# A two-block transformer on one core: loads of the mixing stage by first use, zeros written a stage earlier, and four units on VectorE's ring of banks

## The chip, the core and the metric

The kernel runs on one core of a Trainium2 chip. The metric is the device time of one execution in microseconds, lower is better. The profile is that of one execution on the same core.

## What is computed

Two layers of a first block (pooling in one, forgetting attention in the other, each with memory attention), and then a second block on the 1024 x 1024 rows `x`. The change lies in the second block. Cut to what matters there:

```python
h = _modulate(_rmsnorm(x, norm1_g[l]), shift1, scale1)
z = h @ w_in[l]
zu, zv, zr = jnp.split(z, [GMLP_WIDTH, 2 * GMLP_WIDTH], axis=-1)
y_a = _gmlp_mixer(zu, zv, gmlp_ln_w[l], gmlp_ln_b[l], gmlp_ws[l], gmlp_bs[l])
y_b = _rwkv7_mixer(zr, ...)
y = jnp.concatenate([y_a, y_b], axis=-1) @ w_out[l]
x = x + gate1[:, None, :] * y
h = _modulate(_rmsnorm(x, norm2_g[l]), shift2, scale2)
y = _hier_moe(h, router_group_w[l], ..., w_gate[l], w_up[l], w_down[l])
x = x + gate2[:, None, :] * y
```

`_rwkv7_mixer` is a scan over 1024 tokens with a 64 x 64 state for each of 8 heads. The kernel solves it in 16 chunks of 64 tokens: within a chunk a triangular system is inverted by levels, and between chunks the state goes through one product each. `_hier_moe` sends each token to 2 of 32 experts in blocks of 128 rows; 15 further blocks stand ready for experts with more than 128 rows, and the rows of those must read as zero where nobody writes them.

## The kernel before

The program is a sequence of stages with a barrier between them (`E.run`). Three matter here.

**The RWKV stage** (`stage_rwkv_pairs`) goes over four pairs of heads, c = 0 to 3. A list `script`, written once and walked by every engine, sets the order: for each pair `turn` (transposes), `A` (five chunkwise products), `AV`, five levels of the inversion, and `tail`. Between the levels of pair c stand the steps that prepare pair c + 1 (`front`): three projections, `small`, and after the fifth level `sums`, whose part on VectorE is a chain of 11 operations. So on VectorE `sums` of pair c + 1 stands ahead of `tail` of pair c. In `tail` TensorE makes GH (the solved rows, four banks), MT (two banks, L1640), N (two banks, L1648 and L1649), Q (two banks, L1657) and Yi (two banks, L1664 and L1665).

Apart from that the stage computes the gMLP columns `zu, zv` in 32 *units* of 128 rows by 256 columns (L1575), each 8 matmuls of 128 x 256. The table `fill` puts them at places of the script, one of them at ("GH", c), behind the four GH banks and ahead of MT, and one at ("N", c), behind N. ScalarE copies each unit out of PSUM to `uv_rows` (L1885), SyncE stores it (L1706).

PSUM's eight banks are two rings of four (`class Ring`): `ringA`, mostly emptied by ScalarE, and `ringD`, emptied by VectorE. Banks are handed out in turn; a `take` waits until the take four before it has been freed, and `free` counts in order:

```python
before = self.n - len(self.banks)
return self.banks[self.at[key] % len(self.banks)], (before if before > 0 else None)
```

GH, Yi and all units use `ringA`; MT, N and Q use `ringD`. GH takes all four banks of `ringA`, so the unit behind it waits for ScalarE's first GH copy (L1908); MT waits for the last.

**The mixing stage** (`stage_mix`) works on blocks of 128 tokens, t = 0 to 7, in a software pipeline of NT + 5 rounds: in round t the two state products of block t (`chain`, L2146, reading `s_mt`), then `mix` and `rwkv_rows` of block t - 1, `turn` of t - 2, `out` of t - 3 (the product with `w_out`, L2188 to L2190), norm and router behind. Six streams (`s_uv`, `s_mt`, `s_n`, `s_qt`, `s_yi`, `s_v`) and the rows `x` are loaded for each block, two buffers each. All DMAs are issued by SyncE in program order: first `ws` and the parameters, then blocks 0 and 1, then `w_o` (4 MB), then the zeros for the 15 further expert blocks (L2277, 7680 KB to `y_slots`), then the streams of block 2. VectorE and TensorE wait once, at the start, for the sum of all parameters. GpSimd splits `w_o` into a high and a low part by eight casts (L2301) and eight subtractions (L2303); `out(0)` waits for all.

**The expert stage** follows and reads the weights.

Of the kernel before, what the change touches and what calls it, by code (L numbers as in the profile page):

```python
# [15 lines left out]
P = 128  # L16
D = 1024
# [1287 lines left out]
UVW = 256  # L1305

# [97 lines left out]
def stage_rwkv_pairs(nc, E, A):  # L1404
# [14 lines left out]
    with ExitStack() as st:  # L1419
# [57 lines left out]
        assert sum(fill.values()) == len(units)  # L1477
# [19 lines left out]

        chunks = [(t, slice(q * C, (q + 1) * C)) for t in range(NT) for q in range(2)]
        of = lambda t: slice(t * C, (t + 1) * C)

        with nc.Block() as block:

            @block.tensor
            def _(pe):
# [61 lines left out]
                turns = iter(units)  # L1566

                def fill_(*at_):
                    for _ in range(fill.get(at_, 0)):
                        q, t = next(turns)  # L1570
                        if t == 0:
                            pe.wait_ge(uv_landed, 16 * (q + 1))
                        bank = take(ringA, ("uv", q, t))
                        for d in range(ND):
                            last = nc.tensor.matmul(bank[:, 0:UVW], E.hT[:, d, t * P:(t + 1) * P], w_uv[:, d, :],  # L1575
                                                    start=(d == 0), stop=(d == ND - 1))
                        last.then_inc(ringA.full, 1)
# [97 lines left out]
            def _(sp):  # L1675
# [16 lines left out]
                turns = iter(units)  # L1692

# [5 lines left out]
                def fill_(*at_):  # L1699
                    for _ in range(fill.get(at_, 0)):  # L1700
                        q, t = next(turns)
# [3 lines left out]
                        sp.wait_ge(ringA.free, ringA.nth(("uv", q, t)))  # L1705
# [28 lines left out]
                steps = {"proj": proj, "turn": turn, "A": a_part, "tail": tail, "fill": fill_}  # L1734
# [3 lines left out]
                sp.wait_ge(S_["stored"], 64 * NPAIR)  # L1738
                for i in range(2):
# [4 lines left out]
            def _(pool):  # L1744
# [23 lines left out]

                done(nc.gpsimd.memset(blocksum[:], 1.0))
# [37 lines left out]
            def _(act):  # L1807
# [68 lines left out]
                turns = iter(units)  # L1876

                def fill_(*at_):
                    for _ in range(fill.get(at_, 0)):
                        q, t = next(turns)  # L1880
# [23 lines left out]
                def tail(c):  # L1904
# [4 lines left out]
                    fill_("GH", c)  # L1909
# [12 lines left out]
            def _(dve):  # L1922
# [145 lines left out]
def stage_mix(nc, E, A, rows_in, rows_out, normed_out, y_slots):  # L2068
# [5 lines left out]
    ZW = 256  # L2074
    H = GW // HD
    NR = N_GROUPS + EXPERTS
    with ExitStack() as st:
# [29 lines left out]
        zeros, zeros_set, zeroed = sb("zeros", [P, ZW]), E.sem("zeros_set"), E.sem("slots_zeroed")  # L2107
        w_landed = {x: E.sem("mix_" + x) for x in ("o", "ws", "row")}
# [17 lines left out]
        with nc.Block() as block:  # L2126

            @block.tensor
            def _(pe):
# [63 lines left out]
                def router(t):  # L2193
                    pe.wait_ge(ringA.free, ringA.nth(("t", t, 1)))
                    bank = take(ringD, ("r", t))
# [4 lines left out]
                pe.wait_ge(sems["tril"], 1)  # L2200
                for h in range(2):
                    bank = take(ringA, ("ws", h))
                    for k in range(4):
                        last = nc.tensor.transpose(bank[:, k * P:(k + 1) * P], ws[:, 4 * h + k, :], E.ident[:])
                    last.then_inc(ringA.full, 1)
                pe.wait_ge(small, 16 * 6)
                for t in range(NT + 5):
                    if t < NT:
                        chain(2 * t)
                        chain(2 * t + 1)  # L2210
                    if 1 <= t <= NT:
                        mix(t - 1)
                        rwkv_rows(t - 1)
# [12 lines left out]
            def _(sp):  # L2226
                sp.dma_start(ws[:], A["gmlp_ws_2"][0].rearrange("h t s -> t h s")).then_inc(w_landed["ws"], 16)
                sp.dma_start(bs[:], A["gmlp_bs_cols"]).then_inc(small, 16)
                sp.dma_start(g2[:], A["rwkv_g2_2"][0]).then_inc(small, 16)
                sp.dma_start(rw[:, :, 0:N_GROUPS], A["router_group_w_2"][0].rearrange("(c p) n -> p c n", p=P)).then_inc(small, 16)  # L2230
# [957 lines left out]
```

## Time and profile before

| what | value |
|---|---|
| median of 3 runs | 3264.18 us (3259.43 to 3264.87) |
| the profiled execution | 3260.56 us, span of the profile 3258.8 us |
| TensorE busy | 2914.8 us, 89% of the span |
| VectorE busy | 1735.0 us, 53% |
| ScalarE busy | 1083.0 us, 33% |
| GpSimd busy | 410.1 us, 13% |
| mean granted TensorE clock | 0.936 |
| RWKV stage, mixing stage, expert stage | first DMA at 1666, 2249 and 2516 us |

Times in the views are microseconds from the span's start. PE is TensorE's matmuls, PEld its weight loads, DVE VectorE, ACT ScalarE, POOL GpSimd, SPq the DMA issues of SyncE. The granted clock is a share of 2.4 GHz: 1.00 is that level, 0.50 is 1.2 GHz. A bracket behind a row of the timeline says how long the engine idled before it and for whom.

### The profile page before, as it was taken

How to read it: one execution, taken by the hardware profiler on the slowest of the kernel's cores; microseconds unless marked ns; L12 is line 12 of the kernel's file. 1: busy time of each engine (PE TensorE's matmuls, PEld its weight loads, DVE VectorE, ACT ScalarE, POOL GpSimd, SP SyncE). 2: the span in 40 equal slices, each digit the busy share in tenths (PEclk: the TensorE clock that was granted, in tenths of full speed). 3: DMA queues.
4: the chain of work that ended last, by engine and by line, in shares of the span. 5: the costliest groups of instructions: out<-in, count | busy, mean ns of one | idle time of the engine just before them, and what ended most of it. 6: DMA issues, size and time to landing. Idle time of an engine off the chain costs nothing. (4 is left out here: it accounts for less than half of the span.)

```text
span 3258.8 us, 45746 instructions
## 1 busy us (share of the span) xinstructions
PE 2914.8 (89%) x18548; PEld 2082.4 (64%) x18548; DVE 1735.0 (53%) x2733; ACT 1083.0 (33%) x1690; POOL 410.1 (13%) x334
## 2 busy tenths in 40 slices
PE   7999899898699999998989999996598599999991
PEld 5877544544477777764436677686477477777770
DVE  2223323464356666662325435262665799999984
ACT  2111100122245555451222212132233365666652
POOL 1322000000222222210021010110300000000001
PEclk9999999899799999999989999998688799999995
DMA  4111031652222112113111021014533699999985
GB/s 152 49 42 42 2 140 45 188 182 65 65 59 59 52 53 59 53 33 129 52 55 37 23 68 60 10 56 155 199 120 117 235 398 399 397 399 397 398 310 223
DMA packets 290277, 454.32 MB, mean 139 GB/s; under 512 B 15616, under 2 KB 157440, under 8 KB 290096
## 3 DMA queue, kind: packets, MB, share of 16 engines
q1 hardware_dynamic: 283040, 426.05, 37.3%
q0 software_dynamic: 7056, 25.69, 2.0%
q8 instruction: 133, 2.18, 0.3%
q14 instruction: 48, 0.39, 0.0%
HBM read 389.77 MB, written 61.93 MB: 139 GB/s over the span
## 5 line engine op out<-in xcount | busy, mean ns | idle before, releaser
L677 PE MATMUL psum<-wo,yT 128*128 128x512 f32 x768 | 337.7, 601 | 15.7 <-DMA wo<-in_w_out 15.7
L677 PEld LDWEIGHTS psum<-wo,yT 128*128 128x128 f32 x768 | 147.3, 193 | 196.7 <-issue 180.1
L910 PE MATMUL psum<-x_hi,w_hi 128*128 128x512 f32 x512 | 212.0, 414 | 29.3 <-POOL w_lo L1011 28.6
L1100 DVE TENSOR_TENSOR fox_pT_lo<-psum,fox_pT_hi 128x512 fp32r<-128x512 f32 (+2 forms) x192 | 107.2, 558 | 183.4 <-ACT fox_pT_hi L1039 174.2
L912 PE MATMUL psum<-x_hi,w_lo 128*128 128x512 f32 x512 | 202.0, 394 | 0.0
L911 PE MATMUL psum<-x_lo,w_hi 128*128 128x512 f32 x512 | 201.0, 393 | 0.0
L2797 ACT CAST hi_d<-land_d 128x2048 fp32r<-128x2048 f32 x66 | 122.7, 1908 | 140.1 <-PE psum L2669 140.1
L1526 PE MATMUL psum<-hT,wr 128*128 128x512 f32 x384 | 167.1, 594 | 0.0
L1009 POOL CAST w_hi<-w_land 128x1024 fp32r<-128x1024 f32 x48 | 49.8, 1037 | 909.7 <-DMA w_land<-in_w_in 509.9
L2942 DVE TENSOR_TENSOR lo_d<-land_d,hi_d 128x2048 fp32r<-128x2048 f32 x66 | 148.3, 2289 | 21.5 <-ACT hi_d L2797 21.5
L162 PE MATMUL psum<-x_hi,w_hi 128*128 128x512 f32 x384 | 151.9, 396 | 8.7 <-POOL w_lo L153 8.7
L163 PE MATMUL psum<-x_lo,w_hi 128*128 128x512 f32 x384 | 151.2, 394 | 0.0
L739 DVE SCALAR_TENSOR_TENSOR x_tile<-x_tile,psum 128x512 f32<-128x512 f32 x32 | 22.0, 688 | 242.2 <-PE psum L677 241.7
L2942 DVE TENSOR_TENSOR lo_g<-land_g,hi_g 128x2048 fp32r<-128x2048 f32 x66 | 150.9, 2288 | 0.0
L164 PE MATMUL psum<-x_hi,w_lo 128*128 128x512 f32 x384 | 150.7, 392 | 0.0
L1050 ACT ACTIVATE fox_p<-fox_p,fox_bias 128x256 f32<-128x256 f32 (+7 forms) x128 | 99.6, 778 | 119.9 <-DVE fox_bias L1086 116.3
L1575 PE MATMUL psum<-w_uv,hT 128*128 128x256 f32 x512 | 124.8, 400 | 10.1 <-ACT GH L1908 9.8
L1526 PEld LDWEIGHTS psum<-hT,wr 128*128 128x128 f32 x384 | 72.8, 191 | 87.9 <-issue 87.4
L910 PEld LDWEIGHTS psum<-x_hi,w_hi 128*128 128x128 f32 x512 | 97.1, 190 | 47.9 <-POOL w_lo L1011 30.1
L2797 ACT CAST hi_g<-land_g 128x2048 fp32r<-128x2048 f32 x66 | 125.2, 1898 | 0.8 <-DMA land_g<-in_moe_w_gate 0.8
L2667 PE MATMUL psum<-hi_d,e_h_hi 128*128 128x512 f32 x264 | 117.2, 444 | 6.7 <-DVE e_h_lo L2959 6.7
L1083 DVE CUSTOM_DVE_ANT_0 fox_p<-psum,ncum 128x256 f32<-128x256 f32 (+7 forms) x128 | 97.0, 758 | 48.8 <-PE psum L929 40.2
(482 smaller groups left out, 6435.5 us busy)
## 6 DMA issues: line engine op xcount, KB each, us to landing
land_g<-in_moe_w_gate SPq DMA_DIRECT2D x66, 1024.0 KB, 7.6
land_u<-in_moe_w_up SPq DMA_DIRECT2D x66, 1024.0 KB, 7.5
land_d<-in_moe_w_down SPq DMA_DIRECT2D x66, 1024.0 KB, 9.1
ada<-in_ada_w SPq DMA_DIRECT2D x24, 1024.0 KB, 5.2
y_slots<-yb SPq DMA_DIRECT2D x33, 512.0 KB, 10.0
w<-in_w_in SPq DMA_DIRECT2D x24, 512.0 KB
wo<-in_w_out SPq DMA_DIRECT2D x12, 1024.0 KB
w_land<-in_w_in SPq DMA_DIRECT2D x24, 512.0 KB, 3.8
```

Source lines behind the costliest of these rows:

```text
L162: self.nc.tensor.matmul(bank[:], hi[:, d, :], E.x_hi[:, d, cols], start=(d == 0), stop=False)
L163: self.nc.tensor.matmul(bank[:], hi[:, d, :], E.x_lo[:, d, cols], start=False, stop=False)
L164: last = self.nc.tensor.matmul(bank[:], lo[:, d, :], E.x_hi[:, d, cols], start=False, stop=(d == ND - 1))
L677: last = nc.tensor.matmul(banks[hf][:], E.yT[:, c, t * P:(t + 1) * P], wo[:, c, hf * HALF:(hf + 1) * HALF], start=(c == 0), stop=(c == NY ...
L910: nc.tensor.matmul(bank[:], hi[:, d, :], E.x_hi[:, d, cols], start=(d == 0), stop=False)
L911: nc.tensor.matmul(bank[:], hi[:, d, :], E.x_lo[:, d, cols], start=False, stop=False)
L912: last = nc.tensor.matmul(bank[:], lo[:, d, :], E.x_hi[:, d, cols], start=False, stop=(d == ND - 1))
L1526: last = nc.tensor.matmul(bank[:], w[m % NW][:, d, :], E.hT[:, d, hf * HALF:(hf + 1) * HALF], start=(d == 0), stop=(d == ND - 1))
L1575: last = nc.tensor.matmul(bank[:, 0:UVW], E.hT[:, d, t * P:(t + 1) * P], w_uv[:, d, :], start=(d == 0), stop=(d == ND - 1))
L2667: nc.tensor.matmul(bank, hi_t, hi_w, start=start, stop=False)
L2797: nc.scalar.copy(w_hi[x][:], land[x][:]).then_inc(hi_set[x], 1)
L2942: V.tensor_tensor(w_lo[x][:], land[x][:], w_hi[x][:].bitcast(F32), ALU.subtract).then_inc(lo_set[x], 1)
```

## The change

1. *Mixing stage, loads.* SyncE issues them in another order: streams `n`, `mt`, `uv` of block 0, `ws`, the gMLP norm's rows, and so on; `w_o` behind the streams of block 1, then the gate, the two `x` blocks and the router's parameters. The waits for parameters are split by semaphore and stand in front of the first use. TensorE's transposes of `ws` and ScalarE's copies of them stand behind the first round's own work.
2. *Zeros.* The memset and the write of the zeros move to the RWKV stage. The write is cut into four parts of 1920 KB; SyncE issues one at the fifth level of each pair.
3. *Unit at ("GH", c).* It takes a bank of `ringD` instead of `ringA`, and VectorE copies it out at the head of its `tail` instead of ScalarE. There are four such units.

The table `units_at` only writes down which units stand at which place; the assignment is the same as before.

```diff
...
+        units_at = {at_: [next(turns) for _ in range(fill.get(at_, 0))] for at_ in places}
...
                 def fill_(*at_):
-                    for _ in range(fill.get(at_, 0)):
-                        q, t = next(turns)
+                    ring = ringD if at_[0] == "GH" else ringA
+                    for q, t in units_at[at_]:
                         if t == 0:
                             pe.wait_ge(uv_landed, 16 * (q + 1))
-                        bank = take(ringA, ("uv", q, t))
+                        bank = take(ring, ("uv", q, t))
...
+                def level(c, m):
+                    if m == LEVELS:
+                        if c == 0:
+                            sp.wait_ge(zeros_set, 1)
+                        part = further[:, c * ZEROS:(c + 1) * ZEROS, :]
+                        sp.dma_start(part, zeros[:].rearrange("p (o n) -> p o n", o=1).broadcast_to([P, ZEROS, ZW])).then_inc(zeroed, 16)
...
@@ scalar, tail @@
                             nc.scalar.copy(GH[:, j, 4 * th:4 * th + 4, :], bank.rearrange("p (t n) -> p t n", t=4)).then_inc(ringA.free, 1)
-                    fill_("GH", c)
                     fill_("N", c)
@@ vector, tail @@
+                    for q, t in units_at["GH", c]:
+                        n = q * NT + t
+                        dve.wait_ge(ringD.full, ringD.nth(("uv", q, t)))
+                        if n >= 2:
+                            dve.wait_ge(uv_stored[n % 2], 16 * (n // 2))
+                        V.tensor_copy(uv_rows[n % 2][:], ringD.bank(("uv", q, t))[:, 0:UVW]).then_inc(ringD.free, 1)
                     for q in range(2):
                         dve.wait_ge(ringD.full, ringD.nth(("MT", c, q)))
@@ stage_mix, tensor @@
-                pe.wait_ge(small, 16 * 6)
                 for t in range(NT + 5):
                     if t < NT:
                         chain(2 * t)
                         chain(2 * t + 1)
+                    if t == 0:
+                        turn_ws()
                     if 1 <= t <= NT:
+                        if t == 1:
+                            pe.wait_ge(ringA.free, ringA.nth(("ws", 1)))
                         mix(t - 1)
+                        if t == 1:
+                            pe.wait_ge(small, 32)
                         rwkv_rows(t - 1)
@@ stage_mix, sync @@
-                sp.wait_ge(zeros_set, 1)
-                further = y_slots[EXPERTS * P:SLOTS, :].rearrange("(p b) d -> p (b d)", p=P).rearrange("p (k n) -> p k n", n=ZW)
-                sp.dma_start(further, zeros[:].rearrange("p (o n) -> p o n", o=1).broadcast_to([P, OVER * D // ZW, ZW])).then_inc(zeroed, 16)
...
+                for x in ("n", "mt", "uv"):
+                    load(x, 0)
+                sp.dma_start(ws[:], A["gmlp_ws_2"][0].rearrange("h t s -> t h s")).then_inc(w_landed["ws"], 16)
+                rows(ln_w, "gmlp_ln_w_2", "ln")
+                rows(ln_b, "gmlp_ln_b_2", "ln")
+                load("qt", 0)
...
@@ stage_mix, vector @@
-                dve.wait_ge(w_landed["row"], 16 * 5)
-                dve.wait_ge(small, 16 * 6)
                 V.memset(T[0][:], 0.0).then_inc(sems["T"], 1)
```

How the order changes on the engines. VectorE at the end of a pair of heads (here the first), where `at<-at,lw` is the last operation of the next pair's front, `L<-psum,ident` the two MT banks, `COPY L` the two N banks and `L<-psum,r` the two Q banks. Before:

```order
L1987 TENSOR_TENSOR r<-r,cl 128x1024
L1989 SCALAR_TENSOR_TENSOR at<-at,lw 128x1024
L2035 TENSOR_TENSOR L<-psum,ident 128x8x64 x2
L2039 COPY L<-psum 128x8x64 x2
L2042 TENSOR_TENSOR L<-psum,r 128x8x64 x2
```

And with the change:

```order
L1998 TENSOR_TENSOR r<-r,cl 128x1024
L2000 SCALAR_TENSOR_TENSOR at<-at,lw 128x1024
L2049 COPY uv_rows<-psum 128x256
L2052 TENSOR_TENSOR L<-psum,ident 128x8x64 x2
L2056 COPY L<-psum 128x8x64 x2
L2059 TENSOR_TENSOR L<-psum,r 128x8x64 x2
```

The copy of the unit stands behind the front and ahead of the MT banks.

SyncE in the RWKV stage with the change, from the last weight load of the first pair's levels to that pair's stores:

```order
L1698 DMA wr<-in_w_in 128x8x128 x3
L1745 DMA y_slots<-zeros 128x15x256
L1712 DMA uv_rows_dram<-uv_rows 128x256
L1703 DMA w_uv<-in_w_in 128x8x256
L1712 DMA uv_rows_dram<-uv_rows 128x256
L1733 DMA mt<-L 128x1024
```

The row with the zeros is new; the others stood in this order before.

SyncE in the mixing stage, around `w_o`. Before:

```order
L2256 DMA s_qt<-qt 128x4x128
L2253 DMA s_yi<-yi_rows 128x512
L2253 DMA s_v<-v_rows 128x512
L2262 DMA x_1<-x_rows 128x1024
L2274 DMA w_o<-in_w_out 128x8x1024
L2277 DMA y_slots<-zeros 7680x1x256
L2253 DMA s_uv<-uv_rows_dram 128x1024
L2256 DMA s_mt<-mt 128x4x128
```

And with the change:

```order
L2266 DMA s_v<-v_rows 128x512
L2302 DMA w_o<-in_w_out 128x8x1024
L2303 DMA gate<-gate_rows_dram 128x1024
L2275 DMA x_0<-x_rows 128x1024
L2275 DMA x_1<-x_rows 128x1024
L2306 DMA rw<-in_router_group_w 128x8x4
L2307 DMA rw<-in_router_expert_w 128x8x32
L2308 DMA rb<-in_router_group_b 128x4
L2309 DMA rb<-in_router_expert_b 128x32
L2266 DMA s_uv<-uv_rows_dram 128x1024
L2269 DMA s_mt<-mt 128x4x128
```

The last two rows of each are the streams of block 2. What stands between `w_o` and them is the zeros before, and the gate, the two `x` blocks and the router's parameters now.

## Rows read from the trace of the kernel before

**Rows 1.** Busy time by stretch; after the engines: PEclk, DMA share, GB/s.
```profile
1734.00:2249.00 515.00, 493.11 (x7962) 378.71 (x7960) 233.97 (x251) 121.83 (x210) 58.95 (x40) 0.99 0.14 44
2249.00:2265.00 16.00, 1.97 (x8) 1.57 (x8) 0.27 (x1) 2.45 (x3) 1.42 (x2) 0.50 0.85 219
2265.00:2285.00 20.00, 11.47 (x98) 9.19 (x98) 12.34 (x26) 7.25 (x10) 0.00 (x0) 0.50 1.07 384
2285.00:2311.00 26.00, 0.13 (x2) 0.13 (x4) 8.50 (x8) 1.29 (x3) 23.07 (x14) 0.50 1.06 367
```
**Rows 2.** Timeline of TensorE, start of the mixing stage: start us, us, what.
```profile
2310.87 1.12 PE L2146 MATMUL psum<-T,s_mt 64*64 64x64 f32 x16 [26.52 <-DMA s_mt<-mt]
...
2341.83 0.78 PE L2188 MATMUL psum<-w_o_hi,y2T_hi 128*128 128x512 f32 x1
```
**Rows 3.** Timeline of SyncE's DMA issues, start of the mixing stage.
```profile
2249.38 0.38 SPq L2227 DMA_DIRECT2D ws<-in_gmlp_ws  x1
...
2270.96 0.68 SPq L2274 DMA_DIRECT2D w_o<-in_w_out  x1
...
2273.37 29.43 SPq L2253 DMA_DIRECT2D s_uv<-uv_rows_dram  x1
```
**Rows 4.** DMA issues by line: count, KB each, median us to landing.
```profile
y_slots<-zeros SPq DMA_DIRECT2D x1, 7680.0 KB, 36.7
...
ws<-in_gmlp_ws SPq DMA_DIRECT2D x1, 512.0 KB, 4.3
```
**Rows 5.** TensorE's waits, 1734 to 2249 us: us in total, times, longest.
```profile
PE psum L1575 <- ACT GH L1908: 9.8, 3, 3.3
```
**Rows 6.** Timeline of TensorE, tail of pair 0.
```profile
1863.03 5.41 PE L1575 MATMUL psum<-w_uv,hT 128*128 128x256 f32 x16 [3.27 <-ACT GH L1908]
...
1869.88 0.28 PE L1648 MATMUL psum<-GH,tok_b 64*64 64x64 f32 x2
...
1873.75 3.72 PE L1575 MATMUL psum<-w_uv,hT 128*128 128x256 f32 x16
1877.40 1.73 PE L1657 MATMUL psum<-rbT,GH 64*64 64x64 f32 x58
```
**Rows 7.** Timeline of VectorE, tail of pair 0.
```profile
1876.52 1.28 DVE L2035 TENSOR_TENSOR L<-psum,ident 128x512 f32<-128x512 f32 x2
```
**Rows 8.** Timeline of VectorE: an operation on 128x256 that reads PSUM.
```profile
2312.13 0.42 DVE L2369 TENSOR_TENSOR T<-psum,s_n 128x256 f32<-128x256 f32 x1 [18.28 <-PE psum L2146]
```
**Rows 9.** Timelines of VectorE and TensorE, tails of pairs 1 and 2.
```profile
2000.61 6.77 PE L1575 MATMUL psum<-w_uv,hT 128*128 128x256 f32 x16 [3.27 <-ACT GH L1908]
...
2014.10 1.28 DVE L2035 TENSOR_TENSOR L<-psum,ident 128x512 f32<-128x512 f32 x2
...
2016.28 1.73 PE L1657 MATMUL psum<-rbT,GH 64*64 64x64 f32 x58
...
2140.32 5.20 PE L1575 MATMUL psum<-w_uv,hT 128*128 128x256 f32 x16 [3.27 <-ACT GH L1908]
...
2153.82 1.28 DVE L2035 TENSOR_TENSOR L<-psum,ident 128x512 f32<-128x512 f32 x2
...
2154.55 1.74 PE L1657 MATMUL psum<-rbT,GH 64*64 64x64 f32 x58
```
**Rows 10.** Timeline of GpSimd: first and last of 16 operations that split `w_o`.
```profile
2287.37 1.04 POOL L2301 CAST w_o_hi<-w_o 128x1024 fp32r<-128x1024 f32 x1 [32.53 <-DMA w_o<-in_w_out]
...
2313.41 2.41 POOL L2303 TENSOR_TENSOR w_o_lo<-w_o,w_o_hi 128x1024 fp32r<-128x1024 f32 x1
```
**Rows 11.** Timeline of VectorE beside GpSimd's split, block 0.
```profile
2287.43 1.51 DVE L2413 TENSOR_TENSOR y<-y,gn_w 128x512 f32<-128x512 f32 x1
2288.98 2.71 DVE L2414 TENSOR_TENSOR s_v<-s_v,gn_b 128x512 f32<-128x512 f32 x1
2291.73 1.41 DVE L2415 TENSOR_TENSOR y<-y,s_v 128x512 f32<-128x512 f32 x1
```
**Rows 12.** Timeline of VectorE with GpSimd quiet, block 2.
```profile
2344.28 0.69 DVE L2414 TENSOR_TENSOR s_v<-s_v,gn_b 128x512 f32<-128x512 f32 x1
```

More of the change, by code:

```diff
@@ L1305 @@
 UVW = 256
+ZW = 256
 class Modulation:
@@ L1699, in fill_ @@
                 def fill_(*at_):
-                    for _ in range(fill.get(at_, 0)):
-                        q, t = next(turns)
+                    ring = ringD if at_[0] == "GH" else ringA
+                    for q, t in units_at[at_]:
                         if t == NT - 1 and q + 1 < 2 * GW // UVW:
@@ L1874, in turn @@
                     nc.scalar.copy(E.bonus[:, :, 2 * c:2 * c + 2], bank[:, 0:2 * NT].rearrange("p (t j) -> p t j", t=NT)).then_inc(ringA.free, 1)
-                turns = iter(units)
                 def fill_(*at_):
-                    for _ in range(fill.get(at_, 0)):
-                        q, t = next(turns)
+                    for q, t in units_at[at_]:
                         n = q * NT + t
@@ L2106, in stage_mix @@
         small = E.sem("mix_small")
-        zeros, zeros_set, zeroed = sb("zeros", [P, ZW]), E.sem("zeros_set"), E.sem("slots_zeroed")
-        w_landed = {x: E.sem("mix_" + x) for x in ("o", "ws", "row")}
+        w_landed = {x: E.sem("mix_" + x) for x in ("o", "ws", "ln", "gn", "gate", "router")}
         x_landed = [E.sem(f"x2_landed{i}") for i in range(NX)]
@@ L2198, in router, with turn_ws @@
                     last.then_inc(ringD.full, 1)
[L2200 to L2205, printed above, removed]
-                pe.wait_ge(small, 16 * 6)
+                def turn_ws():
+                    pe.wait_ge(sems["tril"], 1)
+                    for h in range(2):
+                        bank = take(ringA, ("ws", h))
+                        for k in range(4):
+                            last = nc.tensor.transpose(bank[:, k * P:(k + 1) * P], ws[:, 4 * h + k, :], E.ident[:])
+                        last.then_inc(ringA.full, 1)
                 for t in range(NT + 5):
@@ L2273, in _ @@
+                for x in ("qt", "yi", "v"):
+                    load(x, 1)
+                sp.dma_start(w_o[:], A["w_out_2"][0].rearrange("(c p) n -> p c n", p=P)).then_inc(w_landed["o"], 16)
+                sp.dma_start(gate[:], E.gates[:, 0:D]).then_inc(w_landed["gate"], 16)
+                for t in range(NX):
                     load_x(t)
-                sp.dma_start(w_o[:], A["w_out_2"][0].rearrange("(c p) n -> p c n", p=P)).then_inc(w_landed["o"], 16)
-                sp.wait_ge(zeros_set, 1)
@@ L2293, in _ @@
             def _(pool):
-                nc.gpsimd.memset(zeros[:], 0.0).then_inc(zeros_set, 1)
                 pool.wait_ge(w_landed["ws"], 16)
@@ L2309, in got @@
                     return ringA.bank(key)
-                for h in range(2):
-                    nc.scalar.copy(wsT[:, 4 * h:4 * h + 4, :], got(("ws", h)).rearrange("p (h n) -> p h n", h=4)).then_inc(ringA.free, 1)
                 for t in range(NT + 5):
@@ L2323, in _ @@
                         nc.scalar.activation(gdev[:], mv_[:, 1:2], ACT.Sqrt, bias=E.eps_ln[:]).then_inc(sems["dev"], 1)
+                    if t == 0:
+                        for h in range(2):
+                            nc.scalar.copy(wsT[:, 4 * h:4 * h + 4, :], got(("ws", h)).rearrange("p (h n) -> p h n", h=4)).then_inc(ringA.free, 1)
                     if 1 <= t <= NT:
```

69 lines of the change are left out of this document (44 added, 25 removed).

## The prediction

> **What bounds the kernel now.** I read the busy time by stretch first. From 1734 to 2249 us, the stage that solves the RWKV chunks, TensorE works 493 of 515 us at almost full clock, while the DMA engines are used to 0.14 [rows 1]: time that TensorE loses there is lost to the kernel. I then read TensorE's timeline where the mixing stage begins. It computes 128 tokens (a block) at a time. The third block's state product starts at 2310.87 us after 26.52 us of idling for `s_mt`, and the first product with `w_out` at 2341.83 us [rows 2]. SyncE's timeline says why: its first DMA of the stage goes out at 2249.38 us, `w_o` at 2270.96, the zeros behind it, and the third block's `s_uv` then sits 29.43 us in the issue [rows 3]. The zeros are 7680 KB and land 36.7 us after their issue [rows 4]. So this gap is the DMA queue's, and behind it everything up to the first `w_out` product is late.
>
> The third view is TensorE and VectorE beside each other at the end of a pair of heads. In three of the four pairs TensorE idles for ScalarE's GH copies before the unit behind the solved rows, 9.8 us in all [rows 5]. Pair 0: the unit starts at 1863.03 after 3.27 us of idling, the two N banks follow from 1869.88, the next unit at 1873.75 and Q at 1877.40 [rows 6]. VectorE at that time is in the next pair's front, which stands ahead of this tail in its program, and takes up the first MT bank only at 1876.52 [rows 7].
>
> **The change part by part.**
>
> *Unit behind the solved rows on ringD.* The unit no longer waits for ScalarE's GH copies, so it moves up by 3.3 us per pair. But `ringD` has four banks, and the takes are now unit, MT, MT, N, N: the second N bank is the fourth take after the unit and gets the unit's bank. It is free only once VectorE has copied it, and VectorE comes to that copy after the front, where it used to come to MT. Queued behind the waiting N matmuls on TensorE are the next unit, Q and Yi. The copy of 128x256 out of PSUM costs about 0.42 us by the nearest row [rows 8]. Pair 0: the copy ends at 1876.52 + 0.42 = 1876.94, N's second bank starts at about 1877.05 with 0.1 for the signal, one N bank takes (1873.75 - 1869.88) / 2 = 1.9 us, the unit 3.65 us, and Q starts at 1882.6 instead of 1877.40: 5.2 us late. What ScalarE gives back is swallowed by the same wait. Pairs 1 and 2 by the same sum from 2014.10 and 2153.82: Q at 2020.2 instead of 2016.28, and 2159.9 instead of 2154.55, so 3.9 and 5.3 us [rows 9]. Pair 3 has no next front and its unit did not idle: 0. Sum 14.4 us.
>
> To this comes the clock. After an idle stretch of 3.27 us the same unit took 5.41, 6.77 and 5.20 us instead of 3.72 [rows 6, 9], 6.2 us over the three pairs. The new idle stretch is longer, 9 to 10 us: without its own idling the unit starts at 1859.8, and with 3.65 us for it, 1.4 for MT (1863.03 + 5.41 to 1869.88) and 1.9 N's first bank ends at 1866.8 at the earliest, the second starts at 1877. No row shows an idle stretch of this length in this stage, so I bound it: 0 if the clock holds, and N's 1.9 plus the unit's 3.7 at half clock, 5.6 a pair or 16.8, if it is low all through. I take the 6.2 of the nearest rows. Term: **+20.6 us**, between 14.4 and 31.
>
> *Zeros in the RWKV stage.* Four writes of 1920 KB, 5.4 us each at the 367 GB/s of the stretch in which the old one ran [rows 1]. They go out at each pair's fifth level, into queues used to 0.14; the next transfers that anyone waits for are the tail's stores, over 10 us later. Cost 0; without that cover it would be up to 5.4 us a pair. The memset moves ahead of the masks on GpSimd: 0.3 us at most, and not on TensorE's path.
>
> *Mixing stage, loads.* In bytes: ahead of and with `w_o` stand two blocks of streams (3584 KB), `ws` 512, four parameter rows 1024, `g2` 192 and `w_o` 4096, together 9.63 MB, at the 384 GB/s of the stretch 2265 to 2285 [rows 1] 25.1 us. The first transfer landed 4.3 us after its issue [rows 4], of which 1.4 us are its bytes, so 2.9 us of latency come on top: `w_o` lands 28 us after the stage's first DMA. Gate, two x rows and the router's weights (1.7 MB, 4.5 us), the third block's `s_uv` and `s_mt` (2.0 us), and 4 us for the router's small pieces follow (an estimate: the first 16 us moved 219 GB/s [rows 1], 6.9 us less than at 384, of which 2.9 are the latency). The third block then starts at about 39 us instead of 2310.87 - 2249.38 = 61.5: **22.5 us** earlier, with 3 us either way. The first blocks gain too (VectorE waited for all the parameter rows before), but blocks 0 and 1 are then done near 30 us and stand before the same gate, so that gain is not counted again.
>
> *What the earlier `w_o` brings with it.* GpSimd splits `w_o` for 28.5 us, from 2287.37 to 2315.8 [rows 10]. Before, TensorE and VectorE mostly idled meanwhile. Now the split runs from 28 to 57 us or more, and the third block works from 39 us beside it. VectorE's operations with both inputs in SBUF suffer there: three in a row took 1.51, 2.71 and 1.41 us [rows 11], and the middle one takes 0.69 us with GpSimd quiet [rows 12]: 1.2 us more each on average. A block has 12 such operations; some 9 fall before the split's end: 10.8 us, less 1 us that the old third block already lost. I take 10, between 4 and 16. The Trainium skill (SBUF — State Buffer, "Who interferes with whom") says that such an instruction and one of GpSimd that reads SBUF exclude each other for a whole instruction; taken at its worst, a wait of a whole GpSimd instruction each time, it gives the rival "locked" below.
>
> After the first `w_out` product the order of work is the same and a block costs what it did. Term: 22.5 - 10 = **-12.5 us**, between -5 and -21.
>
> **Sum:** 20.6 - 12.5 = +8.1 us. The profiled execution took 3260.56 us around a span of 3258.8 and would take 3268.7; the median of the runs, 3264.18, lies 3.6 us higher. I forecast the median: 3272 us, slower by 0.25%. From no change a measurement of this kernel can tell about 0.2%, 6.5 us.
>
> **The rivals.**
> *Undisturbed split.* VectorE's waits for GpSimd fall where it would have waited for TensorE or ScalarE anyway, and the third block loses next to nothing. It decides from about 0.2 us a conflicting operation. Then 20.6 - 22.5 = -1.9: 3262 us, and with a clock that holds -8: 3256. For it: the conflict is seen on three operations only. Against: VectorE is the engine that is waited for in a block.
> *The unit's move works as drawn.* Were the second N bank not held (VectorE reaching the copy in time), the 9.8 us of idling go and nothing comes: -9.8 - 12.5 = -22: 3242 us. Against it stand 1876.52, 2014.10 and 2153.82 [rows 7, 9], each some 10 us later than N's second bank could start (1866.8 in pair 0).
> *Cold TensorE.* The longer idle keeps the clock at half for N and the unit: +31 - 12.5 = 18.5: 3283 us. For it: the three old units differ by 1.6 us in what they lost.
> *Locked.* Each of the 9 operations waits out a mean GpSimd instruction, 28.5 / 16 = 1.8 us: 16 instead of 10 us, 3278 us.
>
> **How the numbers follow.** Forecast 0.45, undisturbed split 0.24, works as drawn 0.09, cold 0.11, locked 0.11. The predicted time is that of the forecast. The range, 3257 to 3284, holds the forecast's bounds, "cold" and "locked" and most of "undisturbed", and leaves out "works as drawn" and the tails. Slower by over 0.2%: three quarters of the forecast's case, cold and locked, 0.56. Within: the rest of the forecast's and three quarters of "undisturbed", 0.29. Faster: 0.15.
>
> **What would show it.** In the profile after: the unit behind the solved rows follows the solve without idling; the second half of N waits for the VectorE copy of `uv_rows`, some 9 us in each of pairs 0 to 2, and none in pair 3; ScalarE's idle before N does not matter. No zeros in the mixing stage, the third block's product some 39 us after the stage's first DMA, the first `w_out` product some 79 us after it (92.5 before). VectorE's operations in the third block stretched up to 2.7 us. I am wrong if N shows no wait, or if the RWKV stage is not longer by 14 us or more, or if the mixing stage up to the first `w_out` product shrinks by less than 5 or more than 21 us.

## The result, and the profile after

The changed kernel takes 3275.22 us (median of 7 runs, 3270.87 to 3276.2) and the kernel before, on the same chip, 3264.08 us (7 runs, 3259.43 to 3267.55): ratio 1.0033, 95% interval 1.0022 to 1.0045. It is slower, by 11 us where 8 were forecast. The profiled execution took 3275.86 us around a span of 3274.1. Of the kernel before, one execution in the third group of experiments took 4819.97 us at a granted clock of 0.587; it is left out everywhere.

From the first DMA of one stage to the first of the next, the two traces differ like this:

| stretch | before | after | difference | forecast |
|---|---|---|---|---|
| up to the RWKV stage | 1666.3 | 1663.8 | -2.5 | 0 |
| RWKV stage | 583.1 | 608.9 | +25.8 | +20.6 |
| mixing stage, up to the first `w_out` product | 92.45 | 80.1 | -12.4 | -12.5 |
| from that product to the first expert DMA | 173.9 | 178.2 | +4.3 | 0 |
| expert stage and the rest | 743.1 | 743.2 | +0.1 | 0 |

TensorE's waits in the RWKV stage of the changed kernel (us in total, times, longest):

```profile
PE psum L1656 <- DVE uv_rows L2049: 26.5, 3, 8.9
...
PE psum L1648 <- ACT GH L1920: 3.0, 3, 1.1
```

The 9.8 us of waiting for GH [rows 5] are down to 3.0, and 26.5 us of waiting for VectorE's copy of the unit stand in their place, three times, as forecast. TensorE and VectorE in the tail of pair 0 (start, length, operation, in brackets the idle time before it and its releaser):

```profile
1856.29 3.72 PE L1583 MATMUL psum<-w_uv,hT 128*128 128x256 f32 x16
...
1873.58 0.49 PE L1656 MATMUL psum<-GH,tok_b 64*64 64x64 f32 x4 [8.85 <-DVE uv_rows L2049]
...
1877.24 5.56 PE L1583 MATMUL psum<-w_uv,hT 128*128 128x256 f32 x16
1882.73 1.73 PE L1665 MATMUL psum<-rbT,GH 64*64 64x64 f32 x58
```
```profile
1871.97 1.23 DVE L2000 SCALAR_TENSOR_TENSOR at<-at,lw 128x1024 f32<-128x1024 f32 x1
1873.11 0.42 DVE L2049 COPY uv_rows<-psum 128x256 f32<-128x256 f32 x1
1873.44 1.28 DVE L2052 TENSOR_TENSOR L<-psum,ident 128x512 f32<-128x512 f32 x2
1874.64 0.68 DVE L2056 COPY L<-psum 128x512 f32<-128x512 f32 x1
```

Compare [rows 6, 7]. The unit ends at 1860.0, and its bank is copied at 1873.11, when the last operation of the next pair's front (L2000) is through. The copy takes the 0.42 us that were assumed. The second bank of N then takes 3.66 us (1873.58 to 1877.24) where a bank took 1.9 before, and the next unit 5.56 instead of 3.72. The granted clock over these two and after them (busy time of TensorE, its weight loads, VectorE, ScalarE, GpSimd, then PEclk, DMA share, GB/s); it is at the lower level, 0.50 or 1.2 GHz, over all of N's bank, at 0.66 on average over the unit, and back at 2.4 GHz by 1884:

```profile
1873.50:1876.90 3.40, 3.32 (x62) 3.32 (x63) 1.82 (x4) 0.00 (x0) 0.00 (x0) 0.50 0.13 43
1877.30:1882.70 5.40, 5.40 (x17) 4.22 (x16) 0.69 (x1) 0.00 (x0) 0.00 (x0) 0.66 0.00 0
1884.00:1889.00 5.00, 5.00 (x149) 5.00 (x146) 1.31 (x2) 0.58 (x1) 0.00 (x0) 1.00 0.78 236
```

In the mixing stage the third block's state product and the first product with `w_out` come 41.6 and 80.1 us behind the stage's first DMA at 2272.67 (61.5 and 92.45 before, [rows 2]):

```profile
2314.28 1.12 PE L2161 MATMUL psum<-T,s_mt 64*64 64x64 f32 x16 [16.51 <-DMA s_mt<-mt]
...
2352.76 0.78 PE L2203 MATMUL psum<-w_o_hi,y2T_hi 128*128 128x512 f32 x1
```

SyncE no longer sits behind the zeros [rows 3], but on the router's weights, and the third block's `s_uv` goes out 35.6 us into the stage:

```profile
2293.71 10.16 SPq L2307 DMA_DIRECT2D rw<-in_router_expert_w  x1
2303.92 3.87 SPq L2308 DMA_DIRECT2D rb<-in_router_group_b  x1
...
2308.31 0.43 SPq L2266 DMA_DIRECT2D s_uv<-uv_rows_dram  x1
```

GpSimd's split runs from 31.5 to 60.5 us of the stage, and VectorE's operations of the third block beside it are stretched, as in [rows 11]:

```profile
2304.20 1.04 POOL L2330 CAST w_o_hi<-w_o 128x1024 fp32r<-128x1024 f32 x1 [21.26 <-DMA w_o<-in_w_out]
...
2330.85 2.34 POOL L2332 TENSOR_TENSOR w_o_lo<-w_o,w_o_hi 128x1024 fp32r<-128x1024 f32 x1
```
```profile
2319.52 2.23 DVE L2412 TENSOR_SCALAR vn<-vg,g_mv,g_rstd 128x512 f32<-128x512 f32 x1
2321.79 1.40 DVE L2415 TENSOR_TENSOR vn<-vn,gln_w 128x512 f32<-128x512 f32 x1
2323.23 2.72 DVE L2416 TENSOR_TENSOR vn<-vn,gln_b 128x512 f32<-128x512 f32 x1
...
2331.30 1.92 DVE L2437 TENSOR_SCALAR gn_s<-gn_s 128x8 f32<-128x8 f32 x1
```

The four parts of the zeros land 9.1 us (median) after their issue; none of TensorE's longest waits in the RWKV stage is for them.

### The profile page after: what moved, and what is told of

Read it like the earlier page. It is cut to its first block and busy times, and to the rows that moved or that the text cites. A ratio compares the mean times of both kernels' runs of the same rounds, so it can differ in the third digit from the quotient of the medians.

```text
span 3274.1 us, 45754 instructions
## 1 busy us (share of the span) xinstructions
PE 2922.9 (89%) x18548; PEld 2086.6 (64%) x18548; DVE 1741.4 (53%) x2737; ACT 1081.9 (33%) x1686; POOL 411.5 (13%) x334
```

## The experiments

The theory (A): the unit's place on `ringD` costs the RWKV stage all it lost, since its copy stands behind VectorE's front; the zeros bring nearly all that the mixing stage gained. Eleven kernels were run, in three groups (e1 to e4, e5 to e8, e9 to e11), each group on another chip and with its own runs of the kernel before, whose medians were 3262.91, 3262.61 and 3260.15 us. Across groups the ratios are to be compared, and the medians only roughly. A letter names a rival within its own experiment: rival D of e2 and rival D of e6 are different ones.

| run | median us | ratio to before, 95% | RWKV stage | third block | first `w_out` product |
|---|---|---|---|---|---|
| before | | | 583.1 | 61.5 | 92.4 |
| after | 3275.22 | 1.0033 (1.0022 to 1.0045) | 608.9 | 41.6 | 80.1 |
| e1 order and zeros | 3251.44 | 0.9964 (0.9951 to 0.9977) | 585.7 | 41.3 | 79.9 |
| e2 unit alone | 3290.33 | 1.0081 (1.0063 to 1.0099) | 608.0 | 61.1 | 92.0 |
| e3 zeros alone | 3252.99 | 0.9972 (0.9960 to 0.9983) | 588.6 | 40.4 | 84.2 |
| e4 order alone | 3264.84 | 1.0004 (0.9993 to 1.0016) | 584.0 | 63.2 | 93.7 |
| e5 router late | 3245.67 | 0.9953 (0.9940 to 0.9966) | 582.7 | 38.3 | 78.9 |
| e6 unit's copy in front | 3258.03 | 0.9985 (0.9976 to 0.9994) | 589.0 | 41.6 | 79.8 |
| e7 three copies in front | 3237.27 | 0.9924 (0.9911 to 0.9937) | 576.1 | 42.3 | 79.9 |
| e8 no subtractions | 3241.80 | 0.9939 (0.9926 to 0.9952) | 582.2 | 41.2 | 71.7 |
| e9 casts on ScalarE | 3242.21 | 0.9949 (0.9933 to 0.9964) | 581.7 | 40.7 | 75.1 |
| e10 unit on ringA, copies in front | 3246.97 | 0.9959 (0.9944 to 0.9974) | 578.9 | 41.5 | 80.0 |
| e11 all | 3234.46 | 0.9929 (0.9911 to 0.9946) | 570.8 | 38.5 | 76.1 |

The last three columns are from one profiled execution each: the length of the stage, and the start behind the mixing stage's first DMA.

**e1.** The changed kernel, its third part undone.
```diff
-                    ring = ringD if at_[0] == "GH" else ringA
+                    ring = ringA
@@ scalar, tail @@
+                    fill_("GH", c)
                     fill_("N", c)
@@ vector, tail @@
-                    for q, t in units_at["GH", c]:
...
-                        V.tensor_copy(uv_rows[n % 2][:], ringD.bank(("uv", q, t))[:, 0:UVW]).then_inc(ringD.free, 1)
```


> The changed kernel with one of its three parts undone: the unit behind the solved rows goes back to ScalarE's ring and ScalarE's copy, in all four pairs. Load order, split waits and zeros stay as changed. Theory A (the 26.5 us that TensorE waits for VectorE's copy of that unit, with the slower clock behind each wait, is what the RWKV stage lost): from the stage's first DMA to the mixing stage's it takes 583 us again (608.9 in the changed kernel, 583.1 before), the three waits of 8.85 us on VectorE's uv_rows copy are gone, w_out's first product stays about 80 us behind the mixing stage's first DMA, and the kernel takes 3275.2 - 25.8 = 3249 us, 0.995 of the kernel before (3245 to 3254). Rival B (the zeros' four DMAs inside the RWKV stage cost part of the 25.8 us): the stage keeps 588 to 600 us and the total stays at 3254 to 3266. Rival C (the mixing stage's gain is given back once the stage runs into the experts without the slack upstream): total over 3258.

**e2.** The kernel before with that part alone (one line of several; SyncE's, ScalarE's and VectorE's go with it).
```diff
-                        bank = take(ringA, ("uv", q, t))
+                        bank = take(ring, ("uv", q, t))
```


> The kernel before with only the unit behind the solved rows moved to VectorE's ring and VectorE's copy; loads, waits and zeros as before. Theory A: the RWKV stage takes 609 us (583.1 before), three waits of about 9 us on VectorE's copy, the mixing stage as before (first product of w_out 92 us behind the stage's first DMA), total 3264.1 + 25.8 = 3290 us (3286 to 3293), ratio 1.008. Rival D (the unit on VectorE's ring does what it is drawn to do, and the loss came with the zeros or the new waits): 3252 to 3264 us, ratio 0.997 to 1.000.

TensorE's waits in the RWKV stage, e1 and then e2:
```profile
PE psum L1583 <- ACT GH L1920: 9.8, 3, 3.3
```
```profile
PE psum L1653 <- DVE uv_rows L2037: 26.6, 3, 8.9
```
Both came out by theory A within 3 us: e1 is 11.5 us faster than before, e2 27.4 us slower. The unit on `ringD` costs the RWKV stage 23.2 us with the rest of the change (608.9 against 585.7) and 24.9 us without it (608.0 against 583.1), and rivals B, C and D of these two fall. The two other parts are a gain of 0.36%, which the third more than eats.

**e3, e4.** The zeros alone, and the order of the loads with the split waits alone. In e4 the zeros are issued here:
```diff
                 sp.dma_start(rb[:, N_GROUPS:NR], A["router_expert_b_2"].broadcast_to([P, EXPERTS])).then_inc(w_landed["router"], 16)
+                sp.wait_ge(zeros_set, 1)
...
+                sp.dma_start(further, zeros[:].rearrange("p (o n) -> p o n", o=1).broadcast_to([P, OVER * D // ZW, ZW])).then_inc(zeroed, 16)
```


> The kernel before with only the zeros moved: written in four parts by the RWKV stage, gone from the mixing stage; the mixing stage's loads keep their old order and its waits are the old joint ones. Theory A (the 7680 KB of zeros in front of the second block's streams were what held the mixing stage): the third block's first product is 40 to 44 us behind the stage's first DMA (61.5 before, 41.6 in the changed kernel), w_out's first product at 80 to 86 us (92.5 before, 80.1 changed), total 3264.1 minus 6 to 12 = 3252 to 3258 us. Rival E (the order of the loads and the split waits bring at least half of the mixing stage's gain): the first product of w_out at 86 us or later, total 3259 or more.

> The kernel before with only the mixing stage's loads in order of first use and the waits split; the zeros stay in the mixing stage, as the last load ahead of the second block's streams, and the unit on ScalarE's ring. Theory A (order and split waits move work only inside the time that the zeros take anyway): the third block's first product at 58 to 64 us behind the stage's first DMA, w_out's first product at 88 to 95 us, total 3261 to 3266 us. Rival E (they bring at least half of the gain): w_out's first product at 86 us or less, total under 3259.

The third block's product and the first `w_out` product in e3 (its stage begins at 2256.27) and e4 (2253.24):
```profile
2296.64 1.12 PE L2156 MATMUL psum<-T,s_mt 64*64 64x64 f32 x16 [6.02 <-DMA s_mt<-mt]
...
2340.45 0.78 PE L2198 MATMUL psum<-w_o_hi,y2T_hi 128*128 128x512 f32 x1
```
```profile
2316.46 1.12 PE L2145 MATMUL psum<-T,s_mt 64*64 64x64 f32 x16 [38.74 <-DMA s_mt<-mt]
...
2346.94 0.78 PE L2187 MATMUL psum<-w_o_hi,y2T_hi 128*128 128x512 f32 x1
```
Both came out by theory A, and rival E falls. The zeros alone bring 9.9 us. The order alone brings nothing that can be told: e4 has its first blocks done earlier and then idles 38.74 us where the kernel before idled 26.52. On top of the moved zeros the order gets the first `w_out` product from 84.2 to 79.9 us, but e1 and e3 differ in the median by 1.6 us only, less than can be told apart.

**e5.** e1, and the router's four loads behind the third and fourth block's streams.
```diff
-                sp.dma_start(rw[:, :, N_GROUPS:NR], A["router_expert_w_2"][0].rearrange("(c p) n -> p c n", p=P)).then_inc(w_landed["router"], 16)
...
+                    if t == 2:
...
+                        sp.dma_start(rw[:, :, N_GROUPS:NR], A["router_expert_w_2"][0].rearrange("(c p) n -> p c n", p=P)).then_inc(w_landed["router"], 16)
```


> The run with order and zeros as changed and the unit back on ScalarE's ring, and in it the router's four loads issued two blocks later, behind the third and fourth block's streams. In the changed kernel SyncE issues the router's expert weights for 10.16 us and its group bias for 3.87 us, and the third block's uv_rows only behind them, 35.6 us after the stage's first DMA. Theory A (the router's small pieces hold SyncE and so the third block's streams): the third block's first product moves from 41.3 us to about 36 us behind the stage's first DMA, w_out's first product from 79.9 us to 75 to 78 us, total 3246 to 3250 us against 3251.4 of that run. Rival F (the streams then only meet GpSimd's split and the queue elsewhere): w_out's first product stays at 79 to 81 us, total within 2 us of 3251.4.

```profile
2269.38 1.28 SPq L2261 DMA_DIRECT2D s_uv<-uv_rows_dram  x1
2270.71 1.39 SPq L2264 DMA_DIRECT2D s_mt<-mt  x1
...
2273.17 9.66 SPq L2264 DMA_DIRECT2D s_qt<-qt  x1
```
SyncE, from the stage's start at 2248.78, now issues `s_uv` at 20.6 us and sits 9.66 us on another stream, `s_qt` of the same block. So a hold of this length does not need the small pieces of the router; what decides where SyncE is held no run shows. Nor is the hold what the third block waits for in the main: its `s_mt` goes out 21.9 us into the stage and not 35.9 as in e1, 14.0 us earlier, but the product that waits for it starts only 3.0 us earlier (38.3 against 41.3). The first `w_out` product comes 1.0 us earlier (78.9), between the two theories, and the median, 3245.67, lies just below theory A's range. It is 5.8 us below e1, but each is compared with its own runs of before, and the two ratios' intervals overlap: unclear.

**e6.** The changed kernel; in pairs 0 to 2 the unit's copy stands in the middle of the next pair's front.
```diff
@@ vector, sums @@
                     link(dve, V.reciprocal(tmp[:], tmp[:]))
+                    if c > 0:
+                        unit_out(c - 1)
@@ vector, tail @@
-                    for q, t in units_at["GH", c]:
...
+                    if c == NPAIR - 1:
+                        unit_out(c)
```


> The changed kernel with one thing moved: in pairs 0 to 2 VectorE copies the unit behind the solved rows in the middle of the next pair's front, right behind the reciprocal, and not behind the whole front. Same instructions, same rings. Theory A (N's second bank waits only because the copy that frees it stands at the end of VectorE's front): the three waits of 8.85 us before N go, N runs at the fast clock in 1.9 us; Q now waits 3 to 5 us for VectorE's MT copy, as the unit did for GH in the kernel before. The RWKV stage takes 580 to 586 us (608.9 changed, 583.1 before), total 3248 to 3254 us, like the run with the unit on ScalarE's ring. Rival D (the ring of four banks itself is too short with one unit more in it): the stage stays over 595 us and the total over 3262 us.

**e7.** e6, and the MT and N copies too.
```diff
                     link(dve, V.tensor_tensor(K[:], K[:], rate[:], ALU.mult))
+                    if c > 0:
+                        mt_out(c - 1)
...
                     link(dve, V.tensor_tensor(K[:], K[:], e2[:], ALU.mult))
+                    if c > 0:
+                        n_out(c - 1)
```


> The run before, and VectorE's MT and N copies of pairs 0 to 2 stand in the next pair's front too (MT behind k's scaling by the rate, N behind k's product with e). Theory A (behind the solved rows the bound is VectorE's order, since Q waits for the MT copy behind the front): Q starts some 5 us earlier in each of three pairs, the front ends 3 us later, the RWKV stage takes 568 to 578 us, total 3236 to 3248 us. Rival G (the next pair's front is what bounds each pair's end, and lengthening it by 3 us costs what Q gains): the stage takes 580 to 590 us, total 3248 to 3258 us.

**e10.** e7, with the unit back on `ringA` and ScalarE's copy; MT and N stay in the front.
```diff
-                    ring = ringD if at_[0] == "GH" else ringA
+                    ring = ringA
@@ vector, sums @@
-                    if c > 0:
-                        unit_out(c - 1)
```


> The run with VectorE's unit, MT and N copies in the next pair's front (3237.3 us), and in it the unit behind the solved rows goes back to ScalarE's ring and ScalarE's copy; the MT and N copies stay in the front. Theory A (the ring change is worth its 9.8 us of TensorE waiting for GH copies, as the change has it, as soon as VectorE's copies no longer stand behind the front): the three waits of 3.3 us on ScalarE's GH copy come back, the RWKV stage takes 583 to 588 us against 576.1, total 3244 to 3250 us. Rival I (the gain came from the moved MT and N copies alone, and the ring does nothing, because what TensorE waits less there it waits more at the next front): the stage takes 574 to 579 us, total 3234 to 3241 us.

The longest of TensorE's waits for another engine in the RWKV stage, in e6, e7 and e10:
```profile
PE psum L1665 <- DVE L L2059: 12.2, 3, 4.1
```
```profile
PE psum L1648 <- ACT GH L1920: 3.2, 3, 1.1
```
```profile
PE psum L1583 <- ACT GH L1920: 9.5, 3, 3.3
```
Q's first 58 products in pair 0 of e6:
```profile
1875.81 2.99 PE L1665 MATMUL psum<-rbT,GH 64*64 64x64 f32 x58 [4.05 <-DVE L L2059]
```
VectorE in pair 0 of e7, front and copies interleaved:
```profile
1859.84 6.55 DVE L2012 RECIPROCAL tmp<-tmp 128x1024 f32<-128x1024 f32 x1
1866.42 0.42 DVE L1985 COPY uv_rows<-psum 128x256 f32<-128x256 f32 x1
...
1871.44 1.29 DVE L1994 TENSOR_TENSOR L<-psum,ident 128x512 f32<-128x512 f32 x2
...
1875.22 1.29 DVE L2001 COPY L<-psum 128x512 f32<-128x512 f32 x2
```
In e6 the wait before N is gone with nothing changed but the copy's place, so e6's rival D falls: the ring is long enough, the order of VectorE was the fault. But the stage, 589.0 us, is 3 us longer than expected and the median, 3258.03 (0.9985), 4 us above the range. Q waits 4.05 us for the MT copy, which also stands behind the front. That wait was expected; not expected was that it costs clock as well: Q's first 58 products take 2.99, 3.00 and 3.00 us in the three pairs instead of 1.73, 3.8 us in all. In e7 no wait for another engine over 1.1 us is left there, rival G falls, and the kernel is at 0.9924 of the one before, 25 us faster; the changed one was at 1.0033.

e10 puts a price on the unit's ring: with the MT and N copies in the front the unit on `ringA` brings 9.5 us of waiting for GH back, and the kernel stands at 0.9959 (0.9944 to 0.9974) against e7's 0.9924 (0.9911 to 0.9937), 9.7 us in the medians. The total is theory A's; the stage is not: 578.9 us where theory A had 583 to 588 and rival I 574 to 579. The 576.1 of e7 that both were reckoned from was a long one: e11 has the same RWKV code and took 570.8, 8.1 us less than e10 (last section). So by the total, and by e11's stage, rival I falls, and the third part of the change is a gain of its own once VectorE's order fits it. The moved MT and N copies by themselves, e10 against e1, show no clear gain: 0.9959 against 0.9964, with intervals that overlap.

**e8.** e1; GpSimd writes zeros where it subtracted.
```diff
-                    nc.gpsimd.tensor_tensor(w_o_lo[:, d, :], w_o[:, d, :], w_o_hi[:, d, :].bitcast(F32), ALU.subtract).then_inc(wo_split, 1)
+                    nc.gpsimd.memset(w_o_lo[:, d, :].bitcast(F32), 0.0).then_inc(wo_split, 1)
```


> The run with order and zeros as changed and the unit on ScalarE's ring, and in it GpSimd sets w_out's low part to zero where it subtracted before, so the low part of w_out is left out of the product. Theory A (GpSimd's eight subtractions of 2.34 us stretch VectorE's operations of the third block: 2.72 us against 0.69 us): the split ends 8 to 12 us earlier, VectorE's stretched operations of that block go back to 0.42 to 0.69 us apart from those beside the casts, w_out's first product moves from 79.9 us to 70 to 76 us behind the stage's first DMA, total 3242 to 3248 us. Rival F (the block is bound by its streams' landing and the chain of TensorE and VectorE, the stretch only fills waits): w_out's first product stays at 78 to 80 us, total 3249 to 3252 us.

**e9.** e1; the casts on ScalarE.
```diff
@@ gpsimd @@
-                    nc.gpsimd.tensor_copy(w_o_hi[:, d, :], w_o[:, d, :]).then_inc(wo_hi_set, 1)
@@ scalar @@
+                    if t == 2:
+                        act.wait_ge(w_landed["o"], 16)
+                        for d in range(ND):
+                            nc.scalar.copy(w_o_hi[:, d, :], w_o[:, d, :]).then_inc(wo_hi_set, 1)
```


> The run with order and zeros as changed and the unit on ScalarE's ring (3251.4 us), and in it ScalarE makes the eight casts of w_out, in the idle time before the third block's gelu, and GpSimd only the eight subtractions. Theory A (what is left of the split beside the third block costs the block its stretch; the run without subtractions had w_out's first product at 71.7 us against 79.9): the split ends 51 to 54 us behind the stage's first DMA (some 60 there), VectorE's operations behind that are back at 0.4 to 0.7 us, w_out's first product at 74 to 77 us, total 3245 to 3249 us. Rival H (ScalarE's casts hold back its gelu of the third block, or stretch as VectorE's operations do): w_out's first product at 79 us or later, total 3250 or more.

VectorE's operations of the third block in e8 beside GpSimd (the casts run until 2291.5), and ScalarE and GpSimd in e9:
```profile
2290.61 1.40 DVE L2410 TENSOR_TENSOR vn<-vn,gln_w 128x512 f32<-128x512 f32 x1
2292.05 0.69 DVE L2411 TENSOR_TENSOR vn<-vn,gln_b 128x512 f32<-128x512 f32 x1
...
2294.28 0.69 DVE L2421 TENSOR_TENSOR y<-y,gu 128x512 f32<-128x512 f32 x1
```
```profile
2274.01 7.67 ACT L2338 CAST w_o_hi<-w_o 128x1024 fp32r<-128x1024 f32 x8 [4.08 <-DMA w_o<-in_w_out]
```
```profile
2275.20 19.32 POOL L2326 TENSOR_TENSOR w_o_lo<-w_o,w_o_hi 128x1024 fp32r<-128x1024 f32 x8 [21.88 <-ACT w_o_hi L2338]
```
With the third block starting at the same time (41.2 and 41.3 us), the first `w_out` product comes 8.2 us earlier in e8: that is the contention on the third block, less what the casts left of it in e8. e8 leaves the low part of `w_out` out of the product and is no kernel to keep. In e9 the split ends at 51.3 us and 4.7 of the 8.2 us are gained; the median, 3242.21, is 3 us under theory A's range. By the place of the first `w_out` product and by the totals rival F of e8 and rival H fall; whether e9 is faster than e1 is not shown, since the two ratios' intervals overlap.

**e11.** e7, e5 and e9 together.

> All that gained, together: the changed kernel with VectorE's unit, MT and N copies in the next pair's front, the router's loads two blocks later, and w_out's casts on ScalarE. If the gains lie in different stages and add up: RWKV stage 574 to 578 us, w_out's first product 73 to 77 us behind the stage's first DMA, total 3237.3 minus 1 to 4 (router) minus 2 to 6 (casts) = 3228 to 3235 us. If later router loads and ScalarE's casts get in each other's way (the third block's uv_rows lands about when the casts run): w_out's first product at 78 us or later, total 3236 or more.

The first `w_out` product came out (76.1 us), the RWKV stage was 3 us under its range (570.8, see below), and the median, 3234.46, lies within its range and is the lowest of all. But against its own runs of before it stands at 0.9929, e7 at 0.9924: what router and casts add to e7 can't be told from nothing here. In its one trace the later router loads bring nothing on top of the casts: the third block starts at 38.5 us as in e5, but the first `w_out` product comes at 76.1 and not at e9's 75.1. The best version is e7 or e11, 25 to 26 us faster than before.

## Why the prediction was right, point by point

- *N waits for VectorE's copy in pairs 0 to 2, "some 9 us" each, none in pair 3.* Right: 8.85 us three times. e1 and e2 show that it is this part of the change that costs, e6 that the place of the copy does it.
- *14.4 us for the later Q.* Right. From the end of the solved rows' product to Q it took 17.6, 18.9 and 17.5 us before and 26.4, 26.7 and 25.7 after, 24.8 us more in all. Take from that what the clock took after the change (next point), 10.6 us, and 14.2 are left; the 6.2 us of slow clock in the units of before were part of Q's old place in the forecast's sum too. The other 1.0 us of the stage's 25.8 lies elsewhere.
- *6.2 us for the clock, from the units behind 3.27 us of idling.* This is the mis-sized term of the sum. N's second bank took 3.66 instead of 1.9 us three times, and the units 5.56, 5.85 and 5.11 instead of 3.72: 5.3 + 5.4 = 10.6 us. e2 repeats it behind its own three waits: the bank 3.7 us each time, the units 5.62, 5.68 and 5.06. The bounds (0 and 16.8) held it. The nearest rows were of a unit that itself began behind a wait; here N's second bank stands between the wait and the unit and is slowed as well, 5.3 us that those rows don't have. Why the unit behind it was still slow for a part no run shows.
- *Zeros in the RWKV stage cost nothing.* No wait shows them, and e1 and e3, which have them there, are at 585.7 and 588.6 us in the profiled execution against 584.0 in e4, which hasn't; but e5, e8 and e9 have them too and are at 582 to 583. No cost is shown, and one of a few us would not be seen in single executions.
- *Mixing stage, loads.* `w_o` in use 31.5 us behind the stage's first DMA (28), third block at 41.6 (39): 3.5 and 2.6 us late, a gain of 19.9 us for 22.5 forecast, within the 3 us given. e3 shows that the zeros carry this alone (40.4). Of the 4 us set aside for the router's small pieces 3.0 are gone when the four loads go (e5, and 38.5 in e11), though not because SyncE is no longer held.
- *10 us of contention.* From the third block to the first `w_out` product it took 31.0 us before and 38.5 after, and 38.6 in e1 against 30.5 in e8: 8 us. The third block lost 7.5 us against before, where 10 were forecast: 2.5 less, which cancels the 2.6 us that the loads gained less. That the term came out at -12.4 for -12.5 is luck. The working was off in its parts too: not 9 operations at 1.2 us were stretched before the split ended, but five with both inputs in SBUF, 5.7 us more than in the next block, and two `tensor_scalar`, 3.4 us more. The rival "undisturbed split" is refuted. The Trainium skill (SBUF — State Buffer, "Who interferes with whom") has a VectorE instruction with two SBUF inputs contend with a GpSimd instruction that reads SBUF, and not with one that only writes it. The traces agree: 2.72 us beside a subtraction, 1.40 in e8 beside a cast, and 0.69 beside GpSimd's last memset. The same section of the Trainium skill also lists `tensor_scalar` among those that can contend, when its operands meet the conditions of a two-port mode. The trace agrees that it can: beside the split it took 2.23 us on 128x512 and 1.92 us on 128x8, against 0.55 and 0.17 with GpSimd quiet.
- *Nothing after the first `w_out` product.* Off by 4.3 us. TensorE idles as long there as before; what differs is the clock (last section).
- *The other rivals.* "Works as drawn" falls with the wait before N; its price also left out the 6.2 us of clock that go with the old idling, so it should have been -28 and not -22. "Cold" had 5.6 us of clock a pair; measured were 3.6, 3.9 and 3.2: N's bank was at the lower level all through, the unit for a part. "Locked" had 16 us of contention for the 7.5 seen.
- *The total.* The two profiled executions differ by 15.3 us: the 8.1 of the sum, 5.2 more in the RWKV stage, 4.3 more in the later mixing stage, 2.5 less ahead of both, and 0.2 of small differences. The medians differ by 11.1: the profiled execution of before lay 3.5 us under its median, that of after 0.6 above, and where those 4 us lie is not known. So the forecast of 8 missed by 3 in the medians and by 7 in the traces. The direction and the wait behind it were right for the reason given; that the miss in the medians is as small as 3 is in part luck, with 4.4 us short in the clock's term and 4.3 in the later mixing stage.

## What to carry to other kernels

Before work is moved to another ring of banks, look for where the consumer that frees the bank stands in its own engine's program, and count which take reuses that bank; the wait moves from the engine that was slow to the one whose program comes to it late. Where it comes late because of a long chain of its own, the small copies that others wait for belong inside that chain: 3 us of copies a pair, moved into VectorE's front, took the changed kernel from 11 us slower than before to 25 us faster. A wait is paid twice where the clock falls behind it: three waits of 8.85 us came with 10.6 us of slower work. A change of several parts with a small sum can hold a gain and a larger loss: run each part alone before it is kept or dropped.

## What the runs showed of the hardware

**The granted clock dips at different places in executions of the same code, and shifts a stage by 5 us.** The unit behind N in pair 0, with no wait in front of it and the same instructions, in e7 and in e11:
```profile
1873.10 6.01 PE L1583 MATMUL psum<-w_uv,hT 128*128 128x256 f32 x16
```
```profile
1866.78 3.72 PE L1583 MATMUL psum<-w_uv,hT 128*128 128x256 f32 x16
```
In e7 the clock was granted at 0.50 from 1869 to 1873, while TensorE was busy for all of these 4 us with N's 64x64 products. The longest gap of the 10 us before was 1.08 us, ahead of MT, and e11 has it too:
```profile
1865.00:1869.00 4.00, 3.68 (x113) 3.68 (x115) 3.93 (x4) 0.27 (x1) 0.00 (x0) 0.82 0.12 37
1869.00:1873.00 4.00, 4.00 (x84) 3.98 (x81) 3.89 (x6) 0.00 (x0) 0.00 (x0) 0.50 0.02 4
```
The RWKV stage is the same code in e7 and e11 and took 576.1 and 570.8 us; 4.8 us of this lie between the solved rows' product and Q of pair 0 (18.5 against 13.7 us). So a dip does not need a long idle stretch, and a stage's length from one execution is known to some 5 us only; the medians decide the small differences here.

**The 4.3 us behind the first `w_out` product are clock too.** From that product to the first expert DMA TensorE idles 14.4 us before and after, but is busy 159.5 us before and 163.7 after, at a mean granted clock of 0.89 and 0.86. The changed kernel and e1 have the same mixing stage; 62.5 to 87.5 us behind that product, after and then e1:
```profile
2415.26:2427.76 12.50, 11.30 (x109) 10.62 (x107) 6.92 (x15) 6.91 (x13) 0.00 (x0) 0.70 0.42 140
2427.76:2440.26 12.50, 12.50 (x46) 9.54 (x45) 11.09 (x20) 3.23 (x7) 0.00 (x0) 0.75 0.28 88
```
```profile
2392.10:2404.60 12.50, 9.65 (x111) 8.08 (x111) 7.37 (x16) 6.91 (x13) 0.00 (x0) 0.95 0.50 154
2404.60:2417.10 12.50, 12.50 (x54) 10.34 (x53) 10.64 (x20) 3.23 (x7) 0.00 (x0) 0.91 0.25 82
```
0.70 and 0.75 against 0.95 and 0.91, for 178.2 against 173.5 us to the first expert DMA. What sets the pattern stays open. With the unit on `ringD` the stretch took 178.2 (after), 177.7 (e2), 178.0 (e6), 177.8 (e7) and 175.7 us (e11), with it on `ringA` between 172.0 (e9) and 176.6 us (e10). The first lie higher on the whole, though nothing of the unit is left in this stage; no run tells why.
